# Local attention in a two-layer hybrid DiT kernel: scores kept in one pair of PSUM banks, next scores queued behind the transposes

## What is computed

```
# local attention, 8 heads of 64, 4 query blocks of 128, T = 128
s_loc = einsum(q block, keys of block n-1, n, n+1) * scale, masked to |i-j| <= 128
s_ctx = einsum(q block, 256 context keys) * scale
p     = softmax([s_loc, s_ctx, sink])          # one row per query
o     = p[..., :3T] @ v_loc + p[..., 3T:-1] @ v_ctx

# bidirectional retention, 8 heads of 64, no softmax
att = (q @ k^T) * decay table
o   = att @ v, then o * rsqrt(mean(o^2)) * silu(gate)
```

## Time and profile before

| | |
|---|---|
| median of 3 executions | 2634.58 us (2633.2 to 2634.98) |
| profiled execution, its own time | 2635.3 us |
| its span in the profile | 2633.6 us |
| granted TensorE clock, mean over the span | 0.958 |
| PE busy in the span | 2422.1 us (92%) |
| DVE busy | 1430.3 us (54%) |
| ACT busy | 877.6 us (33%) |
| the stage `attention_retention` on PE | 889.55 to 1072.98 us, 183.43 us |

### The profile page before, as it was taken

One profiled execution on the slowest core, in us unless ns is written; L12 is line 12 of the kernel. 1 busy time (PEld: TensorE's weight loads), 2 busy tenths in 40 slices (PEclk: granted clock), 3 DMA queues, 4 the chain that ended last, 5 costly groups with the idle time before them and its releaser, 6 DMA issues.

```text
span 2633.6 us, 31456 instructions
## 1 busy us (share of the span) xinstructions
PE 2422.1 (92%) x11634; PEld 1943.3 (74%) x11634; DVE 1430.3 (54%) x1976; ACT 877.6 (33%) x1287; POOL 125.8 (5%) x212
## 2 busy tenths in 40 slices
PE   5899999999899878999999999999989829999997
PEld 2588888899778534778888878888778427788886
DVE  4577733565553567653357653653565487533334
ACT  1422123444531465442222342222344303422222
POOL 1011200000000111000001000100000000000000
PEclk9999999999999899989999989999989969899998
DMA  7477932355412100122357422652312113222322
GB/s 297 172 272 254 329 108 76 129 161 189 144 64 72 47 1 1 61 100 92 94 183 253 152 74 93 213 202 81 106 57 81 64 48 116 72 92 88 106 78 72
DMA packets 94399, 322.09 MB, mean 122 GB/s; under 512 B 11344, under 2 KB 11760, under 8 KB 93008
## 3 DMA queue, kind: packets, MB, share of 16 engines
q1 hardware_dynamic: 67824, 221.75, 25.0%
q0 software_dynamic: 25456, 97.59, 11.0%
q10 hardware_dynamic: 1008, 1.25, 0.1%
HBM read 312.16 MB, written 8.39 MB: 122 GB/s over the span
## 4 chain that ended last, share of the span: by engine, by line
PE 82%; DVE 9%; ACT 4%; issue 2%; DMA 0%; DVEq 0%; ACTq 0%; POOL 0%; POOLq 0%
PE psum L496 25%; PE psum L497 24%; PE psum L498 24%; PE psum L979 1%; PE psum L520 1%; PE psum L653 1%; DVE spectrum L403 1%; DVE term L396 1%; DVE w_lo L1431 1%; PE psum L835 1%; ACT w_hi L999 1%; PE psum L968 1%; DVE stats L2016 1%; PE psum L855 0%; PE psum L702 0%
## 5 line engine op out<-in xcount | busy, mean ns | idle before, releaser
L496 PE MATMUL psum<-h_hi,w_hi 128*128 128x512 f32 (+1 forms) x2256 | 853.9, 378 | 29.3 <-DVE h_lo L1649 13.3
L498 PE MATMUL psum<-h_hi,w_lo 128*128 128x512 f32 (+1 forms) x2256 | 846.3, 375 | 0.0
L497 PE MATMUL psum<-h_lo,w_hi 128*128 128x512 f32 (+1 forms) x2256 | 846.2, 375 | 0.0
L1431 DVE TENSOR_TENSOR w_lo<-raw,w_hi 128x1024 fp32r<-128x1024 f32 (+2 forms) x442 | 470.6, 1100 | 84.4 <-ACT w_hi L999 81.4
L496 PEld LDWEIGHTS psum<-h_hi,w_hi 128*128 128x128 f32 x2256 | 429.2, 190 | 112.7 <-issue 22.3
L999 ACT ACTIVATE w_hi<-raw 128x1024 fp32r<-128x1024 f32 (+2 forms) x442 | 406.1, 951 | 259.3 <-PE psum L498 232.0
L498 PEld LDWEIGHTS psum<-h_hi,w_lo 128*128 128x128 f32 x2256 | 428.6, 190 | 76.2
L497 PEld LDWEIGHTS psum<-h_lo,w_hi 128*128 128x128 f32 x2256 | 429.0, 190 | 74.7 <-issue 1.0
L496 PE MATMUL psum<-act_hi,w_hi 128*128 128x512 f32 (+1 forms) x880 | 331.2, 376 | 9.3 <-issue 5.2
L498 PE MATMUL psum<-act_hi,w_lo 128*128 128x512 f32 (+1 forms) x880 | 329.6, 375 | 0.0
L497 PE MATMUL psum<-act_lo,w_hi 128*128 128x512 f32 (+1 forms) x880 | 329.5, 374 | 0.0
(11 more groups left out here) (269 smaller groups left out, 1864.5 us busy)
## 6 DMA issues: line engine op xcount, KB each, us to landing
raw<-in_gate_up SPq DMA_DIRECT2D x220, 512.0 KB, 4.2
mod_raw<-in_w_mod POOLq DMA_DIRECT2D x168, 512.0 KB, 5.3
raw<-in_down_a SPq DMA_DIRECT2D x80, 384.0 KB, 3.7
raw<-in_down_b SPq DMA_DIRECT2D x80, 320.0 KB, 3.1
raw<-in_hy_in SPq DMA_DIRECT2D x24, 512.0 KB, 3.4
raw<-in_mix_in SPq DMA_DIRECT2D x22, 512.0 KB, 3.4
filt_dram<-made SPq DMA_DIRECT2D x6, 1024.0 KB, 3.8
filt<-filt_dram POOLq DMA_DIRECT2D x2, 3072.0 KB, 11.1
```

The source lines that it names most:

```text
L496: pe.matmul(out, w_hi[:, slot, c:c + P], hi, start=start, stop=False)
L497: pe.matmul(out, w_hi[:, slot, c:c + P], lo, start=False, stop=False)
L498: return pe.matmul(out, w_lo[:, slot, c:c + P], hi, start=False, stop=stop)
L1431: ins = dve.tensor_tensor(w_lo[:, slot, 0:cols], raw[:, slot, 0:cols], w_hi[:, slot, 0:cols].bitcast(F32), ALU.subtract)
```

## The change

Scores of every unit now go to banks 0 and 1, and transposes of every unit to banks 2 and 3. `score(u)` waits for `scores_read` of the unit before it (DVE has read the banks) instead of `copy_out(u-2)`. `turn(u)` additionally waits for `copy_out(u-1)`. On PE, `score(s+1)` is issued in step `s` right behind `turn(s-1)`, where before it stood at the head of step `s+1`; unit 0 is scored ahead of everything. ACT and DVE keep their order and only address other banks.

```diff
@@ -829,17 +829,18 @@
-                    if u >= 2:
-                        pe.wait_ge(probs_t_ready, u - 1)
-                    a = 2 * (u % 2)
-                    pe.matmul(psum[:, a, 0:(hi - lo) * P], q, k[:, lo * P:hi * P], start=True, stop=True)
-                    pe.matmul(psum[:, a + 1, 0:CTX], q, k[:, SEQ:ALL], start=True, stop=True).then_inc(scores_ready, 1)
+                    if u:
+                        pe.wait_ge(scores_read, u)
+                    pe.matmul(psum[:, 0, 0:(hi - lo) * P], q, k[:, lo * P:hi * P], start=True, stop=True)
+                    pe.matmul(psum[:, 1, 0:CTX], q, k[:, SEQ:ALL], start=True, stop=True).then_inc(scores_ready, 1)
 
                 def turn(u):
-                    a, w = 2 * (u % 2), window(u)[4] // P
+                    w = window(u)[4] // P
                     pe.wait_ge(probs_ready, u + 1)
+                    if u:
+                        pe.wait_ge(probs_t_ready, u)
                     for t in range(w):
-                        ins = pe.transpose(psum[:, a + t // 4, t % 4 * P:t % 4 * P + P], probs[:, u % 2, t * P:t * P + P],
+                        ins = pe.transpose(psum[:, 2 + t // 4, t % 4 * P:t % 4 * P + P], probs[:, u % 2, t * P:t * P + P],
                                            ident[:, :])
@@ -881,8 +882,8 @@
                 for s in range(MIX_STEPS):
-                    if s < UNITS:
-                        score(s)
+                    if s == 0:
+                        score(0)
                     if s - 1 in PAIR_END:
                         sums(PAIR_END.index(s - 1))
@@ -890,6 +891,8 @@
                     if 1 <= s <= UNITS:
                         turn(s - 1)
+                    if s + 1 < UNITS:
+                        score(s + 1)
                     if s % 2 and 3 <= s <= UNITS + 1:
                         pv((s - 3) // 2)
@@ -1275,11 +1278,11 @@
-                    a, w = 2 * (u % 2), window(u)[4]
+                    w = window(u)[4]
...
-                    flat = psum[:, a:a + 2, :].rearrange("p b c -> p (b c)")
+                    flat = psum[:, 2:4, :].rearrange("p b c -> p (b c)")
@@ -2011,8 +2014,8 @@
-                    dve.scalar_tensor_tensor(probs[:, i, 0:own], psum[:, 2 * i, 0:own], QK_SCALE, mask[:, m:m + own], ALU.mult, ALU.add)
-                    seq(dve.tensor_scalar(probs[:, i, own:w], psum[:, 2 * i + 1, 0:CTX], QK_SCALE, None, ALU.mult))
+                    dve.scalar_tensor_tensor(probs[:, i, 0:own], psum[:, 0, 0:own], QK_SCALE, mask[:, m:m + own], ALU.mult, ALU.add)
+                    seq(dve.tensor_scalar(probs[:, i, own:w], psum[:, 1, 0:CTX], QK_SCALE, None, ALU.mult))
```

## The result

| | before | after |
|---|---|---|
| median of five runs on one chip | 2634.58 us (2633.2 to 2636.28) | 2620.86 us (2620.39 to 2622.28) |
| ratio of the times | | 0.995, 95% interval 0.9935 to 0.9964 |
| profiled execution, its own time | 2635.3 us | 2622.28 us |
| its span | 2633.6 us | 2620.6 us |
| `attention_retention` on PE | 889.55 to 1072.98, 183.43 us | 892.50 to 1060.21, 167.71 us |

The changed kernel is faster by 9.5 to 17.1 us by that interval. The forecast was 2618, so it was 2.9 us too low, inside its own range of 2613 to 2623. In the stage the gain was 15.7 us where 16.7 were forecast. The profiled execution took 1.4 us more than the median.

What follows compares the result with a forecast made beforehand. A ring through PE, DVE and ACT set the stage's pace; afterwards PE bounds. Second window 18.7 us shorter, less 3.5 for clock, plus 1.5 at the start: 16.7 gained, 2618 us, own range 2613 to 2623.

Steps and rivals of the forecast that it cites:

- The ring: Undisturbed steps: score, DVE's read, exponentials and `copy_out` form a 5.15 us ring; score leaves it, pair 8.9 us against 10.3.
- The idle time: PE's idle time from `ret_score` of step 4 to `mix_out`, followed step by step: 26.7 us against 33.7 before.
- decay tables, three steps: Steps 5, 12 and 19: tables hold ACT before `normalize`, so PE's `turn` waits 1.1, 1.6 and 1.05 us, 3.7 in all.
- `sums`, four times: Ends of pairs: `sums` directly follows `ret_value` and waits for the squares, 1.25 us each time, 5.0 in all.
- `turn` behind `root`: Ends of pairs: `turn` waits for `root`, 0.43 us as before, 1.65 at the last one, 3.0 in all.
- behind `finish`: Steps 13, 20, 27: DVE's long chain makes `turn`, then `score`, stand 1.9, 3.2 and 1.2 us, 6.3 in all.
- steps 29 to 32: End of the stage, retention run out, only the attention ring left: 1.4 + 1.85 + 1.8 = 5.0 us idle.
- The clock: Half-clock matmuls from step 4 on, 11.7 us before: 3.5 us charged afterwards, with ends 0 and 11.7.
- The start: Before step 4: from step 2 `score` no longer waits for `copy_out`, so step 4 is reached 1.5 us earlier.
- The clock does not come back: Rival, chance 0.20: idle places move but low-clock stretches stay as long; gain 8.5 us, time 2626.
- No change: Rival, chance 0.05: three engines' ring closes over `take(s+1)` behind `normalize(s)` on DVE; time 2632 to 2637 us.
- Slower: Rival, chance 0.06: score stands behind `turn`, so each late `turn` delays it; stage 9 us longer, time 2644.

Runs made afterwards that it cites:

- banks alone: The change's banks and waits, but `score(s)` stays at the head of step `s` as in the kernel before: 2618.03 us, run again 2619.32 us.
- The run with long fillers: The change plus 3, 5, 2 and 3 matmuls that nothing reads, ahead of `turn` of units 13, 20, 29 and 30: 2623.23 us.
- finish late: The change with DVE's `finish` one step later, behind `take`, for the first three pairs of retention heads: 2615.5 us.
- root late: The change with ACT's `root` behind `normalize(s-1)` and PE's `sums` behind `ret_score`: 2619.47 us.
- banks alone, finish late: The change's banks and waits with the score at the head of its step, plus `finish` one step later for the first three pairs: 2610.97 us.
- Place alone: Kernel before, with its banks and waits, but `score(s+1)` issued behind `turn(s-1)`: 2667.18 us.

## Why the prediction was right, and where it was not

*The ring.* Right. The undisturbed pair takes 8.56 us against 8.9 forecast (10.10 before, where I had reckoned with twice 5.15) and PE has no gap in it, and "banks alone" shows the cause: taking `copy_out` out of the ring is enough. The 0.35 us of difference came with the new order: with the score right behind it `turn` takes 0.60 us to the next start and the score 1.17, where my prices from the old order were 0.70 and 1.27; the banks alone, in the old order, take 8.96. The work of PE that I added up from single rows, 113.4 us, carried: 118.58 us busy is 5.2 more, and a mean clock of 0.96 over 145.08 us is a loss of 0.04 x 145.08 = 5.8, near enough for a rounded clock (before 11.7, and by the clock 0.08 x 158.82 = 12.7). The run with long fillers, with 113.5 us of work at a clock of 0.99, says the same.

*The idle time*, 26.7 us forecast, 26.5 measured. The agreement of the sum is in part luck: errors of single terms cancel, and 0.5 us of the measured sum are small gaps that no term names.

| term | forecast, us | measured, us |
|---|---|---|
| decay tables, three steps | 3.7 | 1.02 + 1.77 + 1.43 = 4.2 |
| `sums`, four times | 5.0 | 4 x 1.21 = 4.8 |
| `turn` behind `root` | 3.0 | 0.42 + 0.42 + 0.42 + 1.59 = 2.9 |
| behind `att_out` | 3.0 | 3.3 |
| behind `finish` | 6.3 | 2.10 + 2.94 + 1.66 = 6.7 |
| steps 7 and 15 | 0.7 | 0.2 |
| steps 29 to 32 | 5.0 | 1.10 + 0.23 + 1.88 + 0.69 = 3.9 |

The rows of the change for some of them (idle time in the bracket):

```profile
936.58 1.12 PE L882 MATMUL psum<-full,head_ones 128*128 128x512 f32 x2 [1.21 <-ACT full L1309]
...
965.48 0.77 PE L843 MATMUL psum<-ident,probs 128*128 128x128 f32 x5 [2.10 <-ACT probs L1278]
...
1003.43 1.08 PE L843 MATMUL psum<-ident,probs 128*128 128x128 f32 x5 [2.94 <-ACT probs L1278]
```

The last steps were the worst term. Their first two parts came as forecast (1.4 against 1.10 + 0.23, 1.85 against 1.88); the third, 1.8, came as 0.69. The `pv` ahead of the last `turn` ran at the low clock in the change and took 2.40 us, so that PE came too late to stand; in "finish late" the same `pv` took 1.31 us and `turn` stood 1.62. First the row of the change, then those of "finish late":

```profile
1054.96 2.40 PE L856 MATMUL psum<-probs_t,av 128*64 128x128 f32 x20
```

```profile
1049.70 1.31 PE L856 MATMUL psum<-probs_t,av 128*64 128x128 f32 x20
...
1052.63 0.66 PE L843 MATMUL psum<-ident,probs 128*128 128x128 f32 x4 [1.62 <-ACT probs L1278]
```

So idle time and low clock are not independent terms, as my sum had them.

*Behind `finish`* one statement was wrong, not only a size: "Here the new wait for `scores_read` really bites, since a late `take` now holds the next score." In steps 14 and 21 the score waits for nothing. Of the waits that I named in steps 10, 14, 18 and 21, those of 10 and 18 came, beside short ones in 7, 17, 26 and 29, 2.1 us in all where I had said 3 to 4. The late `take` makes the exponentials and with them `turn` late, and when `turn` is over the banks have long been read. PE's order puts the delay on `turn`, and "finish late" confirms it: with `finish` behind `take` both waits of `turn` are gone. In the order of the banks alone it is otherwise: there the late `take` does hold the next score, 1.27 us with `finish` late.

*The clock.* The direction was right, the size not: 3.5 us charged, 5.2 measured, out of 11.7 before. From step 4 on the change has three low stretches, from about 966, 1004 and 1055 us, where I expected two. The third, near the end of the stage:

```profile
1055.00:1058.00 3.00, 2.97 (x24) 2.57 (x24) 2.76 (x6) 2.15 (x5) 0.00 (x0) 0.50 0.00 0
```

The one I missed is behind `finish` of step 13, whose idle time, forecast at 1.9 us and measured at 2.10, I took for too short. Ahead of it PE had worked without a stop since 959.65. A rule by the length of the gap would not have told me more, since the same stand ends both ways: 2.10 us in the change with a fall and 2.08 in "root late" without, 2.70 in "banks alone" without and 2.71 in "banks alone, finish late" with one. What decides between them is not shown; the two kernels that were profiled twice had their falls at the same places both times. The charge for the clock was a guess between 0 and 11.7 us. Of the page that I had named for the clock, "TensorE: Matmul & The Clock Gate" of the Trainium skill, the literal reading would have charged nothing; these rows speak against it.

*The start.* 1.5 us forecast, 2.0 measured, though the clock in that window was lower than before (0.65 against 0.73). This is luck in part: in five of the nine profiles with the same PE instructions up to step 4 the start took 24.1 us, only 0.5 less than before.

*Rivals.* "The clock does not come back" falls, 5.2 us against 11.7. "No change" falls with the pair of 8.56 us. "Slower" named a real mechanism: the wait of `turn` now stands before the score, and the squares are exposed. "Place alone" shows what this place costs without the banks, and the comparison with "banks alone" shows its cost in the change, 2.4 us in the stage (4.3 us of idle time from step 4 on). What decided against it is what the prediction said, that the score is a step ahead. What the prediction lacked is the split: I priced the two edits as one, and so did not see that the second takes away from the first.

## What to carry to other kernels

When two uses share buffers in turn (scores of one unit, transposes of the one before), look at who must be done before the buffer is free; giving each use its own buffers can take an engine out of the ring at no cost in space. Price each part of such a change alone: here the banks brought all of the 15.7 us, and the new place of the score was right in plain steps and wrong where another engine's chain is exposed, so that the best stage had it mixed (157.57 us). Where a gap of PE is long, reckon that the clock may fall behind it, with a range instead of a number, and look at the engine whose chain makes it late, here DVE with POOL beside it, before moving anything on PE.

## What was not expected of the hardware

- A filler, 512 columns of f32 over all 128 rows, took 0.9 us (three from 965.77 to 968.45). The two matmuls of `ret_score`, as many columns over 64 rows each, take 1.06 us together: their four records at 915.13 last 0.59 to 0.69 us each and lie within 1.13 us, so they run side by side, and half of the pair's time is not the price of one.
- POOL beside DVE: an operation on two 128x512 tiles took 1.65 us instead of 0.69, and one on a single column 1.22 us instead of 0.15. It lengthens the chain of `finish` by 2.35 us (3.88 against 1.53).
- The clock fell behind stands of PE of 2.10 and 2.94 us in the change (0.57 and 0.61 in the four us behind), and work that nobody reads prevented it (1.00 in both). But the same stand can end either way: 1.5 us ahead of `turn` of unit 1 and 2.7 us ahead of `turn` of unit 12 were followed by a fall in one kernel and by none in another.
- The same matmuls of the stage repeat to 0.1 us from one profile to another, while the whole kernel's runs spread by 2 to 10 us. Only two kernels were profiled twice, and where the spread of the runs lies was not looked into.
